# Attention in a two-layer hybrid backbone: where transposed probabilities and value products lie in PSUM

## What is computed

```python
def attend(q, k, v, scale):
    s = jnp.einsum('bqhd,bkhd->bhqk', q, k).astype(jnp.float32) * scale
    p = jax.nn.softmax(s, axis=-1).astype(v.dtype)
    return jnp.einsum('bhqk,bkhd->bqhd', p, v)

def reference(...):
    for l in range(DEPTH):
        ...
        yx, yc = token_mixing(...)          # MLA: latent queries see 256 context + 512 latent keys,
        x = x + mx[:, 5] * yx               # context queries see the 256 context keys only;
        ...                                 # NA: latent queries see an 8x16 window + the context
        if not last:
            xc = xc + mc[:, 5] * yc         # the last layer needs no context queries
```

## Time and profile before

| | |
|---|---|
| median of 3 runs | 2892.04 us (2891.72 to 2895.67) |
| the profiled execution's own time | 2889.44 us |
| its span, first to last instruction | 2887.6 us |
| PE busy, PE weight load busy | 97%, 92% of the span |
| DVE, ACT, POOL busy | 51%, 33%, 9% |
| attention of layer 0, of layer 1 (on the span's clock) | about 813 to 987 us, about 2334 to 2467 us |
| mean granted TensorE clock | 0.996 |

### The profile page before, as it was taken

The page is one execution under the profiler, slowest core; times in us unless marked ns, Lnnn a source line. Parts: engine busy times, 40 slices in busy tenths (PEclk is TensorE's granted clock), DMA queues, the critical chain, the costliest instruction groups (busy, mean ns, idle before and its releaser), DMA issues.

```text
span 2887.6 us, 42480 instructions
## 1 busy us (share of the span) xinstructions
PE 2807.2 (97%) x16327; PEld 2646.7 (92%) x16327; DVE 1482.7 (51%) x2293; ACT 947.4 (33%) x1526; POOL 263.3 (9%) x279
## 2 busy tenths in 40 slices
PE   7999999999988899999999999999999998999999
PEld 5999999989977789999999999999998987888887
DVE  6554355455477665533553555245346587633332
ACT  3221122233388642211222322112224388532231
POOL 1000000031234210000000100000003234000000
PEclk9999999999999999999999999999999999999999
DMA  6433243223100224322442234133223201233333
GB/s 224 135 122 99 82 137 122 82 63 78 32 14 12 79 74 134 124 85 81 137 133 58 88 117 134 55 123 117 72 65 87 58 14 46 81 95 107 90 100 90
DMA packets 361092, 262.99 MB, mean 91 GB/s; under 512 B 11086, under 2 KB 339188, under 8 KB 359952
## 3 DMA queue, kind: packets, MB, share of 16 engines
q1 hardware_dynamic: 359440, 256.86, 29.5%
q10 hardware_dynamic: 896, 4.46, 0.4%
q0 software_dynamic: 640, 0.09, 0.0%
HBM read 255.08 MB, written 2.10 MB: 89 GB/s over the span
## 4 chain that ended last, share of the span: by engine, by line
PE 89%; ACT 4%; DVE 3%; issue 2%; POOL 1%; DMA 0%; SPq 0%; POOLq 0%; ACTq 0%; DVEq 0%
PE pair L427 24%; PE pair L428 24%; PE pair L435 24%; PE pair L1311 2%; PE pair L1313 2%; PE pair L1312 2%; PE pair L682 2%; PE pmid L2109 2%; PE pair L683 2%; PE pair L684 2%; ACT prob L2180 1%; ACT pt_hi L2165 1%; DVE pt_lo L2254 1%; PE psum L2134 1%; PE psum L2136 1%
## 5 line engine op out<-in xcount | busy, mean ns | idle before, releaser
L427 PE MATMUL pair<-h_lo,w_hi 128*128 128x384 f32 (+1 forms) x2656 | 906.4, 343 | 0.7 <-ACT sg L1102 0.4
L428 PE MATMUL pair<-h_hi,w_hi 128*128 128x384 f32 (+1 forms) x2656 | 905.4, 343 | 0.0
L427 PEld LDWEIGHTS pair<-h_lo,w_hi 128*128 128x128 f32 x2656 | 498.5, 188 | 22.8 <-issue 0.6
L428 PEld LDWEIGHTS pair<-h_hi,w_hi 128*128 128x128 f32 x2656 | 498.8, 188 | 21.3
L403 DVE TENSOR_TENSOR w_lo<-w_raw,w_hi 128x1024 fp32r<-128x1024 f32 (+1 forms) x262 | 349.0, 1332 | 324.5 <-ACT w_hi L396 321.3
L435 PE MATMUL pair<-h_hi,w_lo 128*128 128x384 f32 (+1 forms) x2656 | 513.8, 343 | 0.0
L435 PEld LDWEIGHTS pair<-h_hi,w_lo 128*128 128x128 f32 x2656 | 463.4, 188 | 20.6
L396 ACT ACTIVATE w_hi<-w_raw 128x1024 fp32r<-128x1024 f32 (+1 forms) x262 | 296.2, 1131 | 539.8 <-PE pair L435 507.4
L427 PE MATMUL pair<-s_lo,w_hi 128*128 128x384 f32 (+1 forms) x1100 | 377.7, 343 | 0.0
L428 PE MATMUL pair<-s_hi,w_hi 128*128 128x384 f32 (+1 forms) x1100 | 377.2, 343 | 0.0
L949 DVE SCALAR_TENSOR_TENSOR pmid<-mod_raw,cs_rows 128x1024 f32<-128x1024 f32 x256 | 315.3, 1232 | 74.8 <-DMA mod_raw<-in_w_mod_rows 58.1
(11 more groups left out here) (310 smaller groups left out, 3603.3 us busy)
## 6 DMA issues: line engine op xcount, KB each, us to landing
mod_raw<-in_w_mod_rows SPq DMA_DIRECT2D x64, 1024.0 KB, 4.9
w_raw<-in_w_ffn_gate SPq DMA_DIRECT2D x88, 512.0 KB, 3.8
w_raw<-in_w_ffn_up SPq DMA_DIRECT2D x88, 512.0 KB, 3.8
w_raw<-in_w_ffn_down SPq DMA_DIRECT2D x64, 704.0 KB, 4.6
w_raw<-in_w_in SPq DMA_DIRECT2D x32, 512.0 KB, 4.0
w_raw<-in_w_out SPq DMA_DIRECT2D x12, 512.0 KB, 4.2
w_raw<-in_w_q_up SPq DMA_DIRECT2D x8, 576.0 KB, 4.1
mod_first<-in_w_mod ACTq DMA_DIRECT2D x4, 1024.0 KB, 9.2
```

The costliest lines, as they stand in the source:

```text
L427: eng.matmul(dst, wh, rl, start=k == 0, stop=False)
L428: eng.matmul(dst, wh, rh, start=False, stop=False)
```

## The change

The transposed probabilities no longer have a fixed place. All parts of all chunks are numbered in one sequence (`turn_no`), and part number n goes to bank n % 3 of three: the two banks of `pmid` and the second bank of `psum2`. The transposes of a part wait until `pt_lo` of the part three before it is done. The value product of a pair of chunks is done in one piece, in the odd step, always in the first bank of `psum2`; so it waits until DVE has finished the output of the pair before (`a_out` one higher than before). On ACT the copy of a value product (L2173 before) moves behind the exponential of its step. DVE's order of work is the same as before. Three semaphores of the latent part are gone: `a_t`, `a_pth` and `a_ptl` count parts.

```diff
+        def turn_no(l, c):
+            return ATT_C0[l] + c + latent_parts(l, c)
+        TURN_PLACES = [pmid[:, 0:512], pmid[:, 512:1024], psum2[:, 512:1024]]
+        def turned_at(number, a, b):
+            return TURN_PLACES[number % 3][:, 0:b - a].rearrange("p (k q) -> p k q", q=P)
...
+        def turn_part(eng, l, c, m):
+            keys = chunk_info(l, c)[4]
+            a, b = keys[m]
+            number = turn_no(l, c) + m
+            eng.wait_ge(a_exp, ATT_C0[l] + c + 1)
+            wait_if(eng, a_ptl, number - 2)
+            for k in range(a // P, b // P):
+                last = eng.transpose(turned_at(number, a, b)[:, k - a // P, :], prob[:, c % 3, k * P:(k + 1) * P], ident[:, :])
+            last.then_inc(a_t, 1)
...
+        def weigh_values(eng, l, b):
...
+            wait_if(eng, a_out, c0 // 2 + b)
+            eng.wait_ge(a_rsum, c0 + 2 * b + 2)
+            for h in range(2):
+                eng.transpose(psum2[:, (2 + h) * P:(3 + h) * P], stat[:, (2 * b + h) % STATS, 2:3].broadcast_to([P, P]),
+                              ident[:, :])
+            eng.wait_ge(a_ptl, turn_no(l, 2 * b + 2))
...
+            both = psum2[:, 0:2 * P].rearrange("p (c q) -> p c q", c=2)
+            for k in kc:
...
 in attention_pe, for s in range(n + 4):
-                if s >= 4:
-                    b, part = (s - 4) // 2, s % 2
...
-                        wait_if(eng, a_out, c0 // 2 + b - 1)
...
+                if s < n:
+                    attention_scores(eng, l, s)
+                for m in range(parts):
+                    turn_part(eng, l, s - 2, m)
+                if s >= 5 and s % 2:
+                    weigh_values(eng, l, (s - 5) // 2)
 in attention_act, for s in range(n + 5):
                     eng.wait_ge(a_max, c0 + s + 1)
-                    wait_if(eng, a_t, c0 + s - 2)
+                    if s >= 3:
+                        eng.wait_ge(a_t, turn_no(l, s - 2))
                     eng.activation(prob[:, s % 3, a:b], pair[s % 2][:, a:b], ACT.Exp, ...)
+                if s >= 5 and s % 2 and s < n + 4:
+                    b = (s - 5) // 2
...
+                    eng.wait_ge(a_pv, c0 // 2 + b + 1)
+                    eng.activation(y_f[r, i if kind == "mla" else 4 + i, q0:q0 + 2 * P], psum2[other, 0:2 * P],
+                                   ACT.Copy).then_inc(a_copied, 1)
```

More of the change, by code:

```diff
@@ L375, in program @@
         bias_hi_done, bias_lo_done, ident_ready = sem("bias_hi_done"), sem("bias_lo_done"), sem("ident_ready")
-        a_latent_t, a_latent_hi, a_latent_lo = (sem(f"a_latent_{k}") for k in ("t", "hi", "lo"))
         tt_loaded = [sem("tt_loaded0"), sem("tt_loaded1")]
@@ L2062, in wait_if, with attention_scores @@
                 eng.wait_ge(semaphore, value)
+        def attention_scores(eng, l, s):
+            c0 = ATT_C0[l]
+            kind, i, j, q0, keys = chunk_info(l, s)
+            g, new = att_group(l, s)
+            qh, ql, kh, kl = att_set[g % 2]
+            rows = slice(0, QK) if kind == "mla" else slice(0, 2 * NA_DIM)
+            if new:
+                eng.wait_ge(a_lo, ATT_SPLITS * l + splits(g)[0] + len(splits(g)[1]))
+                if kind == "na":
+                    eng.wait_ge(na_stacked, 48 * (NA_HEADS * l + g - MLA_HEADS + 1))
+            wait_if(eng, a_exp, c0 + s - 1)
+            for a, b in keys:
+                dst, q, d = pair[s % 2][:, a:b], slice(q0, q0 + P), moved(kind, q0, a)
+                eng.matmul(dst, qh[rows, q], kh[rows, a + d:b + d], start=True, stop=False)
+                if kind == "mla":
+                    eng.matmul(dst, qh[rows, q], kl[rows, a:b], start=False, stop=False)
+                last = eng.matmul(dst, ql[rows, q], kh[rows, a + d:b + d], start=False,
+                                  stop=not (biased(l, s) and a < SEQ))
+            if biased(l, s):
+                first, a = BIAS_FIRST[q0 // P], keys[0][0]
+                eng.wait_ge(bias_lo_done, bias_tables(l, s))
+                for table in (na_hi, na_lo):
+                    last = eng.matmul(pair[s % 2][:, a:SEQ], ident_r[:, :], table[:, j, first:first + SEQ - a],
+                                      start=False, stop=table is na_lo)
+            last.then_inc(a_s, 1)
@@ L2073, in attention_pe @@
                     eng.wait_ge(v_free, TOK // P * (l + 1))
+                parts = len(chunk_info(l, s - 2)[4]) if 2 <= s < n + 2 else 0
                 if s < n:
[L2075 to L2110, removed]
@@ L2221, in attention_pool, with turned_lo @@
                        .then_inc(y_lo_done, 1)
+        def turned_lo(eng, l, c, m):
+            kind, _, _, q0, keys = chunk_info(l, c)
+            a, b = keys[m]
+            number, d = turn_no(l, c) + m, moved(kind, q0, a)
+            eng.wait_ge(a_pth, number + 1)
+            eng.tensor_tensor(pt_lo[:, (a + d) // P:(b + d) // P, c % 4, :], turned_at(number, a, b),
+                              pt_hi[:, (a + d) // P:(b + d) // P, c % 4, :].bitcast(F32), ALU.subtract).then_inc(a_ptl, 1)
         def attention_dve(eng, l):
```

83 lines of the change are left out of this document (27 added, 56 removed).

## The result

The changed kernel takes 2902.70 us, the median of six runs (2901.45 to 2908.03); the kernel before, beside it, 2891.81 (2889.88 to 2895.67). The ratio is 1.004, with a 95% interval of 1.0029 to 1.005: **slower by 10.9 us**. The profiled execution took 2902.31 us, its span is 2900.5, its mean granted clock 0.996 as before.

What follows compares the result with a forecast made beforehand. PE was taken to be held by 24.0 us of `pt_lo` waits, and layer 1's pairs by DVE's chain. Terms +7.1 -3.0 -0.6 -1.5 +1.2 -1.7 +0.8 +3.4 gave +5.7, so 2897.5 us at the median, range 2886 to 2904.

Steps and rivals of the forecast that it cites:

- the forecast's own case: Whole kernel: slower, at 2893 to 2901 us; chance 0.45.
- Layer 1, MLA: +7.1: Layer 1's MLA heads: product moves behind DVE's chain, pairs take 5.88 or 5.62 us, +0.51 for each of 14 pairs.
- -0.3 for its start: Start of both layers, where transposes wait without outputs beside them: -0.6 us for the two together.
- Layer 0, MLA: -3.0: Layer 0's MLA heads: third transpose bank brings heads to 13.8 to 14.2 us, 0.43 less for each of seven.
- NA of layer 0 and its end: -1.5 and +1.6: Layer 0: NA heads and the change from MLA gain 1.5 us; last product waiting for its bank costs 1.6.
- NA of layer 1 and its end: +1.2 and +1.8: Layer 1: NA pairs lose 0.1 to 0.4 us, half hidden, +1.2; last product waiting for its bank costs 1.8.
- Clock: -1.7 and +0.8: Half chances: two low-clock stretches in layer 0 go, -1.7 us; one comes at layer 1's end, +0.8.
- A: Rival, faster: each of 41 `pt_lo` waits loses 0.43 us, layer 1's chain does not bind; 2878 us, chance 0.17.
- B: Rival, much slower: layer 1's waits let the clock fall, 1.7 us each; four falls give 2904 us, chance 0.13.
- C: Rival, no sizeable change: gains and losses are half, the ends stay; 2892 + 2 to 4 us, chance 0.25.

Runs made afterwards that it cites:

- e7: Changed kernel with the value product split in odd steps: reciprocals and first half between latent and context transposes, second half behind; 2887.76 us, ratio 0.9993.
- e8: Changed kernel with DVE's output addition and multiplication ahead of the maximum only in the first step of each layer-0 head; 2899.65 us, ratio 1.0034.
- e3: Changed kernel with the whole value product between the latent and the context transposes in odd steps; 2893.88 us, ratio 1.0009.
- e4: Changed kernel with DVE's output addition and multiplication ahead of the even step's maximum everywhere; 2905.85 us, ratio 1.0045.
- e9: Changed kernel with the edits of e3 and e8 together; 2902.11 us, ratio 1.0037.
- e13: The same kernel as e7, run again beside the kernel before; 2888.13 us, ratio 0.9991.

## Why the prediction was right in kind and too low

Forecast 2897.5 (2886 to 2904), measured 2902.7: inside the range, near its end. By its mechanism it is the forecast's own case (slower, by the product that moved behind DVE's chain), though above the 2893 to 2901 that I gave to it. Of the profiled time, attention was to lose 5.7 us and lost 11.1. That the time stayed in the range is partly luck: layer 1 came out 3.9 us below its terms and layer 0 8.4 above. By the steps:

- **Layer 1, MLA: +7.1, and -0.3 for its start.** The mechanism is right to the hundredth: pairs of 5.88 and 5.62 forecast, 5.87 and 5.60 measured, with the wait at the fifth transpose. So are its terms: by the distance of starts PE stands 0.78 and 0.52 us there (forecast 0.80 and 0.55), and what it does besides is 5.08 (forecast 5.07; e7's pair without a wait is 5.05). The stage lost 4.8, not 6.8. Twelve pairs lost 0.49 each, 5.8 in all; 1.1 less comes from the first pair and from the meeting with the NA heads, where PE now waits 0.74 us for `vn_both` instead of 1.63.
- **Layer 0, MLA: -3.0, and -0.3 for its start.** This is where it failed: +2.6. The sentence was "Elsewhere in a layer the single bank costs nothing: a product ends at the end of an odd step, its copy, addition and multiplication are done by the next `pt_lo` of an even step, and the next product starts a scores block and a T later." I had read it off two steps of layer 1, where all chunks have six transposes. In layer 0 every sixth and seventh step is short. There the next product comes too early for the multiplication, and the step takes 3.52 to 3.68 us instead of 2.98, in seven heads 4.2 us. e8, which takes just that away, shows it.

  The rest of the head is as forecast. From 865.44 to 880.36, across the step shown above, a head takes 14.92. Take off, by the distance of starts, 1.10 and 0.79 for the two waits for `pt_lo`, 0.32 by which one T is late, and the 0.69 of that step: 12.0 are left, PE's own work in the forecast. Without that step four heads take 13.95 to 14.4, where I wrote 13.8 to 14.2. The two heads with bias tables take 14.9, low clock taken off, with a wait of 1.61 us for an exponential that I had not seen, but they took 15.3 before.

  What was too large is the gain: I had 0.43 a head, from two heads of the kernel before, and over these six heads it is 0.23, 1.2 us less. 4.2 + 1.2 is 5.4 of the 5.9 that were missed. The rest lies with the clock: each kernel has one stretch of 0.50 in this stage, from 925.8 before and from 883.4 after, and what they cost is known to about half a microsecond.
- **NA of layer 0 and its end: -1.5 and +1.6.** Measured +2.6. The same short step, four times in this stage, costs 1.7 of it (e8's are that much shorter). The end itself is as written: bank, 0.7 us of product, projection.
- **NA of layer 1 and its end: +1.2 and +1.8.** Measured +1.1. The new waits are there (3.0 us more for `pt_lo`, 1.9 for the last bank), but PE waits 2.6 us less for what the trace calls issue and 0.8 less for POOL's operands than before.
- **Clock: -1.7 and +0.8.** Three stretches in attention before and three after; nothing. One stretch costs between nothing (last section) and 1.6 us: by so much the changed kernel's head with a bias table and a stretch (17.15) is longer than the one without (15.59).
- **The rivals.** A (faster, 2878) needed layer 1's pairs at 5.1 to 5.4. e7 and e3 give exactly these, from another place of the product; so A's waits were worth 3.9 (e7) to 5.4 us (e3, which has no low clock there, while e7 and the kernel before have one stretch each) in layer 0's MLA heads and 2.3 in layer 1's, not the 18 of its count. B fell: the granted clock of layer 1's MLA window is 1.00 with thirteen waits in it. C left attention 2 to 4 us longer, not 11.

The sum by stages: +2.6 +2.6 +4.8 +1.1 is 11.1 in attention (forecast 5.7), and the rest between the layers.

The rule that I had weighed there, from the Trainium skill, "Perfetto Trace Analysis", section "Matmuls" of "Optimizing Tensor Performance" (independent matmul groups rotate through PSUM banks), was nearer than I gave it credit for. It holds for the values wherever a product comes before the bank is empty. In this case that is one step in six of layer 0 and the ends, 14 waits of 8.0 us, not every pair.

## What to carry to other kernels

Before joining or moving a piece of work, ask what it stood beside. Half a value product beside the chain ACT, DVE, PE hid it; behind the chain it was added to it, and a third bank could not give that back. Half of it put into the new gap (e7) turned 11 us of loss into some 3.5 of likely gain. And a wait is measured by the distance of two starts: the idle time in a row's brackets was 0.16 us short of it here, so that three waits a head could pass for half a microsecond of work.

When a buffer becomes single, walk through **every** kind of step for its release, the shortest first, not the one in the timeline that happens to be open. And in an engine's fixed order a result that comes earlier makes another one late: move it only where the engine has just been idle, and look at who waits for what it was moved past (e4, e9).

## What the runs showed of the hardware

Whether TensorE's clock falls at a given place is not fixed by the program. e7 and e13 are the same kernel. In both, PE waits at the same place between the layers. First e7:

```profile
2182.13 0.50 PE L1365 MATMUL pmid<-pool_hi,w_hi 128*128 128x512 f32 x1 [2.40 <-DVE pool_lo L1683]
```

Its windows around it (granted clock third from the right):

```profile
2172.00:2184.00 12.00, 9.60 (x43) 7.64 (x42) 10.91 (x16) 6.66 (x12) 4.13 (x6) 1.00 0.58 150
2184.00:2196.00 12.00, 12.00 (x54) 9.94 (x54) 6.33 (x10) 3.97 (x6) 6.29 (x6) 1.00 0.21 62
```

e13, the wait:

```profile
2182.52 0.80 PE L1365 MATMUL pmid<-pool_hi,w_hi 128*128 128x512 f32 x1 [2.46 <-DVE pool_lo L1683]
```

and the windows:

```profile
2172.00:2184.00 12.00, 9.54 (x40) 7.54 (x39) 10.80 (x17) 6.73 (x13) 4.29 (x3) 0.92 0.56 144
2184.00:2196.00 12.00, 12.00 (x51) 9.89 (x50) 5.96 (x9) 2.17 (x4) 4.81 (x7) 0.94 0.23 69
```

Behind 2.40 us of waiting the clock stayed at 1.00, behind 2.46 it fell for a stretch, and the part between the layers took 1349.4 and 1350.7 us. Nor does a stretch always cost time: e13 has one more in layer 0's NA stage (0.97 against 1.00), and the stage takes 55.0 us in both. So a difference of one or two such stretches between two profiles says nothing of an edit, the stages' last microsecond is not explained here, and the medians of several runs decide.
